# Second attention of a two-block transformer: the last value panel moved behind the query panels and cut in two halves, the orders of TensorE, VectorE and ScalarE around it rewritten

## The chip, the cores and the metric

The kernel runs on one core of one Trainium2 chip. The metric is the device time in microseconds (us); less is better. A core has five engines that work through separate queues and meet at semaphores: TensorE (PE, matrix products, with its weight loads shown as PEld), VectorE (DVE), ScalarE (ACT), GpSimd (POOL) and SyncE (SP, which here only issues transfers).

## The reference, cut to what matters

The program computes two transformer blocks on 512 tokens of width 1024. The first is a mixer with attention and convolution and a large expert layer. The second, where the change lies, is a sliding-window attention with sinks and a gated feed-forward layer:

```
proj = h @ w_in                                     # 1024 query, 256 key, 256 value columns
s = einsum(q, k) * 64 ** -0.5 - slope * dist        # blocks of 128 queries x 256 keys, 16 heads
m = max(max(s), sink);  p = exp(s - m)
denom = sum(p) + exp(sink - m)
o = einsum(p / denom, v)
x = x + o @ w_out
x = x + swiglu_ffn(rms_norm(x), w_gate_up, w_down)
```

## The kernel before, in words

Every weight matrix comes as panels of 128 x 1024 values. For each panel ScalarE writes a rounded copy (`whi`), VectorE writes the rest (`wlo`, line 1674), and TensorE makes 24 products of 128x128 by 128x512 (lines 551 to 553, three for each of eight slices). `whi` and `wlo` have two slots each. So the copy of panel p waits for the counter `used`, that is for the last product of panel p - 2; in the second attention this copy is `swa_panel_hi(p)` on ScalarE (the activation in line 1096), followed by `swa_panel_lo(p)` on VectorE.

The second attention has twelve panels, numbered 0 to 11 by position: one of keys, one of values, four of queries, the second one of keys, and then before the change the second one of values and four of queries. Its softmax goes through sixteen groups n of four heads and one block of queries; two groups make a pair m. Each group passes through all three engines:

- `swa_scores(m)`, TensorE, line 946: scores of a pair into the PSUM banks 4 to 7. From the second pair on it waits until VectorE has read the whole pair before (`bias2`).
- `bias_tiles(n)`, ScalarE, line 1526: the distance penalty of two heads. VectorE doesn't begin group 0 before the tiles 0 to 3 are there (`dve.wait_ge(bias_ready, NH2 // 2)`).
- `swa_bias(n)`, VectorE, lines 2405 to 2412: scores plus penalty, with the row maxima.
- `swa_exp(n)`, ScalarE, lines 1538 and 1540: the exponentials and their sums.
- `swa_norm(n)`, VectorE, lines 2417 to 2423: division by the sum.
- `swa_turn(n)`, TensorE, line 958: transposes the probabilities. It waits for `swa_norm(n)` and for the copy of the turned group n - 1.
- `swa_out(n)`, ScalarE, line 1548 (for n = 11 `swa_turned` on VectorE, line 2441): copies the turned group out of PSUM.
- `swa_values(m)`, TensorE, line 978, and then `swa_hi(m)` on ScalarE and `swa_lo(m)` on VectorE: the products with the values, stored in two parts.

The groups of the first key panel are n = 0 to 7, those of the second n = 8 to 15. `turn_v` (line 932) transposes a value panel, `value2` and `value2_out` store it. `out_part` makes the first products with `w_out` from the parts that are ready. The order of all this is written out by hand, once for each engine; each engine takes its list from top to bottom and stands still at a wait. The functions that the change touches, and their callers:

Of the kernel before, what the change touches and what calls it, by code (L numbers as in the profile page):

```python
# [28 lines left out]
KT = D // P  # L29
# [24 lines left out]
U = MOD1  # L54
# [20 lines left out]
SPLIT = 2  # L75
BANKS = 4
SWB = (0, 2, 3, 1, 0, 2, 3, 3, 3, 3, 3, 3)
SW_ORDER = (0, 2, 4, 5, 6, 7, 1, 3, 8, 9, 10, 11)
ZEROS = 32
ATT = NH * TT  # L80
DT = TT - 1
# [76 lines left out]
def build(nc, panels, mod2_d, small, xT_d, ctxT_d, rope_d, keys_d, dist_d, w_d, ge_d, out):  # L158
    with ExitStack() as ctx:
# [201 lines left out]
        def r_of(g):  # L361

            return g - U if g < EV else g - U - NK
# [172 lines left out]
        def _(pe):  # L536
# [387 lines left out]
            def swa_panel(p):  # L924
                first = p == 0
                panel(SW + p, p % 4, ps[:, SWB[p], :], a_hi, a_lo, r_of(SW) + (p + 1 if p < 7 else p + 4), (h_ready, 3 * KT) if first else None,
                      (lambda k: norm_stat(3, k, bank=1)) if first else None)

            def turn_v(u, bank):
                pe.wait_ge(v2_feat, u + 1)  # L930
                for s in range(TT):
                    last = pe.transpose(ps[:, bank, s * P:(s + 1) * P], v2_feat_sb[:, u, s * P:(s + 1) * P], ident)
                last.then_inc(v2_turned, 1)
# [3 lines left out]
            def swa_scores(m):  # L937

                b, kt, half = groups[2 * m]
                if m:  # L940
                    pe.wait_ge(bias2, 8 * m)
                for r in range(4):
                    for half in range(2):
                        rows_ = slice(half * HD2, (half + 1) * HD2)
                        dst = ps[:, 4 + 2 * half + r // 2, (r % 2) * 256 + (P if b == 0 else 0):(r % 2) * 256 + 256]
                        last = pe.matmul(dst, q2[rows_, kt * 4 + r, b * P:(b + 1) * P],
                                         k2[rows_, kt, max(b - 1, 0) * P:(b + 1) * P], start=True, stop=True)
                last.then_inc(sc2, 1)

            def swa_turn(n):  # L950
                b, kt, half = groups[n]
                tiles = (1,) if b == 0 else (0, 1)
                pe.wait_ge(pn2, n + 1)
                if n:
                    pe.wait_ge(ptc2, n)
                for s in tiles:
                    for r in range(4):
                        last = pe.transpose(ps[:, s, r * P:(r + 1) * P], s2[:, n % 6, r * 256 + s * P:r * 256 + (s + 1) * P], ident)
                last.then_inc(pt2, 1)

            def swa_values(m):

                b, kt, half = groups[2 * m]
                tiles = (1,) if b == 0 else (0, 1)
                pe.wait_ge(ptc2, 2 * m + 2)
                if m == 0:
                    pe.wait_ge(v2_done, 2)
                elif m < 3:
                    pe.wait_ge(o2, m)
                else:  # L970
                    pe.wait_ge(o2, m - 1)
                if m == 3:
                    pe.wait_ge(bank_free, r_of(SW) + 16)
                for s in tiles:
                    for half in range(2):
                        rows_ = slice(half * HD2, (half + 1) * HD2)
                        kv = 2 * kt + half
                        last = pe.matmul(ps[rows_, values_bank(m), :], v2[:, b - 1 + s, kv * HD2:(kv + 1) * HD2],
                                         p2T[:, 2 * ((2 * m + half) % 3) + s, :],
                                         start=(s == tiles[0]), stop=(s == 1))  # L980
                last.then_inc(pv2, 1)


            def out_part(u, first, count):

                if first == 0:
                    pe.wait_ge(lo_ready, SO + u + (1 - U))
                    pe.wait_ge(bank_free, r_of(SO) + u + 1)
                    pe.wait_ge(bias2, 4 * len(groups))
                    pe.wait_ge(o2, TT)  # L990
                if first == 4:
                    pe.wait_ge(o2, 2 * TT)
                for k in range(first, first + count):
                    last = split3(ps[:, 4 + u, :], u, k, b_hi[:, k, :], b_lo[:, k, :], k == 0, k == KT - 1)
                if first == 4:
                    last.then_inc(used, 1)
# [16 lines left out]
            swa_scores(1)  # L1013
            swa_panel(8)
            swa_turn(0)
            turn_v(1, 2)
            swa_scores(2)
            swa_turn(1)
            swa_panel(9)
            swa_turn(2)  # L1020
            swa_values(0)
            swa_scores(3)
            swa_turn(3)
            swa_panel(10)
            swa_turn(4)
            swa_values(1)
            swa_turn(5)
            swa_panel(11)
            swa_turn(6)
            pe.wait_ge(bank_free, r_of(SW) + 16)  # L1030
            swa_scores(4)
            swa_values(2)
            swa_turn(7)
            swa_scores(5)
            swa_values(3)
            swa_scores(6)
            swa_turn(8)
            swa_turn(9)
            swa_scores(7)
            swa_values(4)  # L1040
            swa_turn(10)
            swa_turn(11)
            out_part(0, 0, 2)
            swa_values(5)
            swa_turn(12)
            out_part(0, 2, 2)
            swa_turn(13)
            out_part(1, 0, 2)
            swa_values(6)
            swa_turn(14)  # L1050
            out_part(1, 2, 1)
            swa_turn(15)
            out_part(1, 3, 1)
            swa_values(7)
            out_part(0, 4, 4)
            out_part(1, 4, 4)
            for k in range(2, KT):
# [33 lines left out]
        def _(act):  # L1091
# [464 lines left out]
            for n in range(3):  # L1556
                bias_tiles(n)
                swa_panel_hi(6 + n)
            bias_tiles(3)
            bias_tiles(4)  # L1560
            swa_exp(0)
            swa_panel_hi(9)
            swa_exp(1)
            swa_exp(2)
            swa_panel_hi(10)
            swa_out(0)
            swa_exp(3)
            swa_out(1)
            swa_exp(4)
            swa_exp(5)  # L1570
            swa_panel_hi(11)
            swa_out(2)
            swa_hi(0)
            swa_out(3)
            bias_tiles(5)
            swa_exp(6)
            swa_out(4)
            swa_panel_hi(12)
            swa_hi(1)
            swa_exp(7)  # L1580
            swa_out(5)
            bias_tiles(6)
            bias_tiles(7)
            swa_out(6)
            swa_hi(2)
            swa_out(7)
            swa_exp(8)
            swa_exp(9)
            swa_hi(3)
            swa_exp(10)  # L1590
            swa_out(8)
            swa_exp(11)
            swa_out(9)
            swa_exp(12)
            swa_exp(13)
            hi_next(0, SO, 0)
            swa_hi(4)
            swa_out(10)
            swa_exp(14)
            swa_exp(15)  # L1600
            swa_hi(5)
            swa_out(12)
            swa_out(13)
            swa_hi(6)
            swa_out(14)
            swa_out(15)
            swa_hi(7)

# [60 lines left out]
        def _(dve):  # L1669
# [759 lines left out]
                dve.tensor_tensor(b_lo[:, kt * 4:kt * 4 + 4, at], ps[:, values_bank(m), :].rearrange("p (r t) -> p r t", r=4),  # L2429
                                  f32(b_hi[:, kt * 4:kt * 4 + 4, at]), ALU.subtract).then_inc(o2, 1)  # L2430

            def pair_bias(m):
                swa_bias(2 * m)
                swa_bias(2 * m + 1)

            def swa_turned(n):
                dve.wait_ge(pt2, n + 1)
                dve.wait_ge(pv2, (n - 3) // 2 + 1)
                first = 1 if groups[n][0] == 0 else 0
                to = 2 * (n % 3)  # L2440
                dve.tensor_copy(p2T[:, to + first:to + 2, :], ps[:, first:2, :]).then_inc(ptc2, 1)

            def pair_norm(m):
                swa_norm(2 * m)
                swa_norm(2 * m + 1)

            query2(2, 4)
            dve.tensor_scalar(less_sinks[:, :], col("sinks", 0, NH2), -1.0, None, ALU.mult).then_inc(fold_g, 1)
# [6 lines left out]
            swa_panel_lo(8)  # L2455
            dve.wait_ge(fold_g, 3)
            dve.wait_ge(bias_ready, NH2 // 2)
            pair_bias(0)
            value2(1, 7)
            swa_panel_lo(9)  # L2460
            pair_bias(1)
            pair_norm(0)
            query2(4, 8)
            swa_panel_lo(10)
            value2_out(1, 2)
            pair_bias(2)
            pair_norm(1)
            query2(5, 9)
            swa_panel_lo(11)
            pair_norm(2)  # L2470
            swa_lo(0)
            pair_bias(3)
            query2(6, 10)
            residual(4, 4)
            swa_panel_lo(12)
            swa_lo(1)
            pair_norm(3)
            query2(7, 11)
            dve.wait_ge(bias_ready, NH2)
            pair_bias(4)  # L2480
            swa_lo(2)
            pair_bias(5)
            pair_norm(4)
            swa_lo(3)
            pair_bias(6)
            pair_norm(5)
            pair_bias(7)
            swa_lo(4)
            swa_turned(11)
            pair_norm(6)  # L2490
            lo_next(0, SO, 0)
            swa_lo(5)
            pair_norm(7)
            swa_lo(6)
            swa_lo(7)

# [216 lines left out]
```

## Time and profile before

| | |
|---|---|
| median of 3 runs | 2474.28 us (2472.31 to 2475.38) |
| profiled execution, time | 2492.27 us |
| profiled execution, span from first to last instruction | 2490.5 us |
| TensorE busy in the span | 97% |
| VectorE, ScalarE, GpSimd busy | 68%, 38%, 30% |
| granted TensorE clock, mean | 0.990 |

The span is the time from the first to the last instruction of the one profiled execution; 1.8 us lie around it. The busy share counts an engine as busy while an instruction runs on it; times of instructions are from the start of the span. The second attention begins at about 1942 us of it and ends, with its output panels, at about 2114 us. The granted clock is 1.00 for 2.4 GHz and 0.50 for 1.2 GHz.

### The profile page before, as it was taken

The page shows a single profiled execution, that of the slowest core. Times are in us where ns is not written, and L with a number is a line of the kernel's source. Part 1 is how long each engine was busy: PE and PEld are TensorE (multiplying, and loading weights), DVE is VectorE, ACT ScalarE, POOL GpSimd, SP SyncE. Part 2 cuts the span into 40 slices and gives each one's busy share as a digit, 9 for nine tenths or more (in the row PEclk, how much of TensorE's full clock was granted, in tenths as well). Part 3 has the DMA queues.
Part 4 walks back from the last instruction along what each step waited for, and adds up shares of the span by engine and source line. Part 5 has one row for each costly group of instructions (what it writes and reads, how often), then busy time and mean ns, then how long its engine had stood idle before and what let it go on. Part 6 is the DMA issues. An engine that isn't in the chain of part 4 may idle for free.

```text
span 2490.5 us, 34880 instructions
## 1 busy us (share of the span) xinstructions
PE 2420.3 (97%) x11986; PEld 2062.4 (83%) x11986; DVE 1696.0 (68%) x3261; ACT 935.0 (38%) x1436; POOL 741.3 (30%) x646
## 2 busy tenths in 40 slices
PE   6999999998999999999999999999999989999998
PEld 5887787786888887888888899999999767888886
DVE  4987878787667776778632378888888785444434
ACT  5225842523233333333333333333333474222232
POOL 0000000000036665667675357777741000000000
PEclk9999999998999999999999999999999999999999
DMA  6235813453244444444445689999998212232321
GB/s 270 93 98 186 283 60 127 160 190 132 90 156 143 140 152 135 144 144 148 132 148 181 225 281 365 360 365 359 359 360 292 70 43 68 93 100 93 97 97 68
DMA packets 179146, 436.26 MB, mean 175 GB/s; under 512 B 33392, under 2 KB 82544, under 8 KB 178672
## 3 DMA queue, kind: packets, MB, share of 16 engines
q1 hardware_dynamic: 123984, 331.74, 39.1%
q0 software_dynamic: 34816, 67.41, 7.7%
q10 hardware_dynamic: 20256, 36.06, 3.9%
q8 instruction: 38, 0.62, 0.1%
q14 instruction: 52, 0.43, 0.1%
HBM read 371.48 MB, written 61.01 MB: 174 GB/s over the span
## 4 chain that ended last, share of the span: by engine, by line
PE 83%; DVE 7%; issue 1%; ACT 1%; another core or an unknown queue 1%; ACTq 0%; DVEq 0%
PE ps L551 17%; PE ps L553 17%; PE ps L552 17%; PE ps L897 9%; PE ps L895 9%; PE ps L896 8%; DVE ar L1727 1%; PE ps L794 1%; DVE wlo L1674 1%; PE ps L760 1%; PE ps L869 1%; DVE ar L1789 1%; DVE tiny L1903 1%; PE ps L784 1%
## 5 line engine op out<-in xcount | busy, mean ns | idle before, releaser
L2610 POOL DMA_INDIRECT w_scratch<-ar x384 | 419.2, 1092 | 932.1 <-DVE wlo L2122 823.5
L551 PE MATMUL ps<-b_hi,whi 128*128 128x512 f32 x1312 | 513.3, 391 | 4.6 <-DVE wlo L2120 4.4
L553 PE MATMUL ps<-b_hi,wlo 128*128 128x512 f32 x1312 | 511.5, 390 | 0.0
L552 PE MATMUL ps<-b_lo,whi 128*128 128x512 f32 x1312 | 511.1, 390 | 0.0
L1674 DVE TENSOR_TENSOR wlo<-raw,whi 128x1024 fp32r<-128x1024 f32 x235 | 287.4, 1223 | 272.7 <-ACT whi L1096 203.4
L895 PE MATMUL ps<-a_hi,whi 128*128 128x384 f32 x1016 | 340.8, 335 | 7.5 <-DVE a_lo L2304 5.2
L896 PE MATMUL ps<-a_lo,whi 128*128 128x384 f32 x1016 | 340.2, 335 | 0.4 <-issue 0.4
L897 PE MATMUL ps<-a_hi,wlo 128*128 128x384 f32 x1016 | 340.2, 335 | 0.2 <-issue 0.2
L551 PE MATMUL ps<-a_hi,whi 128*128 128x512 f32 x808 | 322.1, 399 | 0.9 <-DVEq L1884 0.6
L553 PE MATMUL ps<-a_hi,wlo 128*128 128x512 f32 x808 | 315.1, 390 | 0.0
L552 PE MATMUL ps<-a_lo,whi 128*128 128x512 f32 x808 | 315.1, 390 | 0.0
L551 PEld LDWEIGHTS ps<-b_hi,whi 128*128 128x128 f32 x1312 | 246.8, 188 | 57.4 <-issue 6.1
L553 PEld LDWEIGHTS ps<-b_hi,wlo 128*128 128x128 f32 x1312 | 246.5, 188 | 51.6
L552 PEld LDWEIGHTS ps<-b_lo,whi 128*128 128x128 f32 x1312 | 246.8, 188 | 50.9
L1096 ACT ACTIVATE whi<-raw 128x1024 fp32r<-128x1024 f32 x168 | 177.2, 1055 | 294.6 <-PE ps L553 183.4
L2588 POOL DMA_INDIRECT ar<-panels,ar x128 | 150.5, 1176 | 173.3 <-DVE nt L2320 97.7
L895 PEld LDWEIGHTS ps<-a_hi,whi 128*128 128x128 f32 x1016 | 191.4, 188 | 8.9 <-DVE a_lo L2304 5.5
L896 PEld LDWEIGHTS ps<-a_lo,whi 128*128 128x128 f32 x1016 | 191.4, 188 | 1.4 <-issue 1.4
L897 PEld LDWEIGHTS ps<-a_hi,wlo 128*128 128x128 f32 x1016 | 191.3, 188 | 0.0
L2595 POOL DMA_INDIRECT ar<-gelu_scratch,ar x128 | 171.1, 1337 | 49.4 <-issue 38.7
L551 PEld LDWEIGHTS ps<-a_hi,whi 128*128 128x128 f32 x808 | 152.1, 188 | 37.4 <-issue 4.4
L552 PEld LDWEIGHTS ps<-a_lo,whi 128*128 128x128 f32 x808 | 152.0, 188 | 33.5 <-issue 2.9
(298 smaller groups left out, 3470.2 us busy)
## 6 DMA issues: line engine op xcount, KB each, us to landing
raw<-panels SPq DMA_DIRECT2D x302, 512.0 KB
late<-panels SPq DMA_DIRECT2D x128, 512.0 KB
w_scratch<-rstd SPq DMA_DIRECT2D x32, 768.0 KB, 10.7
ar<-w_scratch SPq DMA_DIRECT2D x128, 192.0 KB
ar<-gelu_scratch SPq DMA_DIRECT2D x128, 192.0 KB
ar<-mod SPq DMA_DIRECT2D x32, 512.0 KB
gelu_scratch<-ar ACTq DMA_DIRECT2D x64, 256.0 KB
gelu_scratch<-sq ACTq DMA_DIRECT2D x32, 256.0 KB
```

The source lines that it names most:

```text
L551: pe.matmul(bank, w_h, hi[:, k, :], start=(k == 0), stop=False)
L552: pe.matmul(bank, w_h, lo[:, k, :], start=False, stop=False)
L553: last = pe.matmul(bank, w_l, hi[:, k, :], start=False, stop=(k == KT - 1))
L760: pe.matmul(ps[:, b, :], qT[:, h, t * P:(t + 1) * P], kT[:, hu, 0:T], start=True, stop=True)
L895: pe.matmul(ps[:, d, 0:cols], w_h, hi[:, at, 0:cols], start=first, stop=False)
L896: pe.matmul(ps[:, d, 0:cols], w_h, lo[:, at, 0:cols], start=False, stop=False)
L897: end = pe.matmul(ps[:, d, 0:cols], w_l, hi[:, at, 0:cols], start=False, stop=last)
L1096: act.activation(whi[:, u % SPLIT, :], raw[:, u % RAW, :], ACT.Copy).then_inc(hi_ready, 1)
L1674: dve.tensor_tensor(wlo[:, u % SPLIT, :], src, f32(whi[:, u % SPLIT, :]), ALU.subtract).then_inc(lo_ready, 1)
L2588: nc.gpsimd.indirect_dma_start(v_rows[:, s % VS, :], None, v_table, bass.IndirectOffsetOnAxis(vals[:, column(s)].bitcast(U32), 0)).then_in ...
L2595: nc.gpsimd.indirect_dma_start(g_pick[:, s:s + 1], None, gelus_, bass.IndirectOffsetOnAxis(offs[:, column(s)], 0)).then_inc(gpick_in[h % 2 ...
L2610: nc.gpsimd.indirect_dma_start(experts, bass.IndirectOffsetOnAxis(offs[:, k:k + 1], 0), vals[:, k:k + 1], None)\
```

## The change

The value panel that stood at position 7 now stands at position 11, the query panels move up by one, and TensorE makes its products in two halves (`last_value_half`) with scores and a transpose between them. `turn_v(1, ...)` and with it the store of the values move behind them. The value product of pair 0 waits only for the first value panel, that of pair 3 for both. Beside this all three lists have a new order. The diff, cut:

```diff
-SW_ORDER = (0, 2, 4, 5, 6, 7, 1, 3, 8, 9, 10, 11)
+SW_ORDER = (0, 2, 4, 5, 6, 7, 1, 8, 9, 10, 11, 3)
...
                 if m == 0:
-                    pe.wait_ge(v2_done, 2)
+                    pe.wait_ge(v2_done, 1)
...
                 if m == 3:
-                    pe.wait_ge(bank_free, r_of(SW) + 16)
+                    pe.wait_ge(v2_done, 2)
...
+            def last_value_half(half):
+
+                if half == 0:
+                    pe.wait_ge(lo_ready, SW + 11 + (1 - U))
+                    pe.wait_ge(bank_free, r_of(SW) + 15)
+                for k in range(4 * half, 4 * half + 4):
+                    last = split3(ps[:, SWB[11], :], 3, k, a_hi[:, k, :], a_lo[:, k, :], k == 0, k == KT - 1)
+                if half:
+                    last.then_inc(used, 1)
```

TensorE's list from the second scores to the second output panel, the part that changes:

```diff
             swa_scores(1)
             swa_panel(8)
             swa_turn(0)
-            turn_v(1, 2)
             swa_scores(2)
             swa_turn(1)
             swa_panel(9)
+            swa_scores(3)
             swa_turn(2)
             swa_values(0)
-            swa_scores(3)
             swa_turn(3)
             swa_panel(10)
             swa_turn(4)
+            pe.wait_ge(bank_free, r_of(SW) + 15)
+            swa_scores(4)
             swa_values(1)
+            last_value_half(0)
+            swa_scores(5)
             swa_turn(5)
-            swa_panel(11)
+            last_value_half(1)
             swa_turn(6)
-            pe.wait_ge(bank_free, r_of(SW) + 16)
-            swa_scores(4)
             swa_values(2)
             swa_turn(7)
-            swa_scores(5)
-            swa_values(3)
+            turn_v(1, 3)
             swa_scores(6)
             swa_turn(8)
+            swa_values(3)
             swa_turn(9)
             swa_scores(7)
+            swa_turn(10)
             swa_values(4)
-            swa_turn(10)
             swa_turn(11)
-            out_part(0, 0, 2)
+            out_part(0, 0, 4)
...
```

ScalarE's list, its first part:

```diff
             for n in range(3):
                 bias_tiles(n)
                 swa_panel_hi(6 + n)
+            swa_panel_hi(9)
             bias_tiles(3)
+            swa_panel_hi(10)
             bias_tiles(4)
             swa_exp(0)
-            swa_panel_hi(9)
             swa_exp(1)
+            bias_tiles(5)
             swa_exp(2)
-            swa_panel_hi(10)
             swa_out(0)
+            swa_panel_hi(11)
             swa_exp(3)
             swa_out(1)
             swa_exp(4)
             swa_exp(5)
-            swa_panel_hi(11)
+            bias_tiles(6)
             swa_out(2)
...
```

VectorE's list, its first part (`pair_bias(m)` was `swa_bias(2 * m)` and `swa_bias(2 * m + 1)`, `pair_norm` likewise):

```diff
             dve.wait_ge(bias_ready, NH2 // 2)
-            pair_bias(0)
-            value2(1, 7)
+            swa_bias(0)
+            swa_bias(1)
+            query2(4, 7)
+            swa_norm(0)
+            swa_bias(2)
+            swa_bias(3)
+            swa_norm(1)
+            query2(5, 8)
             swa_panel_lo(9)
-            pair_bias(1)
-            pair_norm(0)
-            query2(4, 8)
+            swa_norm(2)
+            swa_bias(4)
+            swa_bias(5)
             swa_panel_lo(10)
-            value2_out(1, 2)
-            pair_bias(2)
-            pair_norm(1)
-            query2(5, 9)
+            residual(4, 1)
+            query2(6, 9)
+            swa_norm(3)
...
```

Three places in the built order. First ScalarE where the copies of the panels 8, 9 and 10 stand (`whi<-raw`), with the penalty tiles (`ar<-ar,sm`), the table load and the exponentials of group 0 and 1 (the rows that wait for `nmx2`). Before:

```order
L1096 ACTIVATE whi<-raw 128x1024 [waits used,landed0]
L1526 ACTIVATE ar<-ar,sm 128x256 x4
L1538 ACT_TABLE_LOAD
L1538 ACTIVATE ar,tiny<-ar,tiny 128x256 [waits nmx2]
L1538 ACTIVATE ar,tiny<-ar,tiny 128x256 x3
L1540 ACTIVATE tiny<-tiny 128x4
L1096 ACTIVATE whi<-raw 128x1024 [waits used,landed1]
L1538 ACTIVATE ar,tiny<-ar,tiny 128x256 [waits nmx2]
```

The same place of the change, where lines stand ten numbers further down (line 1106 is 1096 of before, 1536 is 1526, 1548 is 1538):

```order
L1106 ACTIVATE whi<-raw 128x1024 [waits used,landed0]
L1106 ACTIVATE whi<-raw 128x1024 [waits used,landed1]
L1536 ACTIVATE ar<-ar,sm 128x256 x2
L1106 ACTIVATE whi<-raw 128x1024 [waits used,landed2]
L1536 ACTIVATE ar<-ar,sm 128x256 x2
L1548 ACT_TABLE_LOAD
L1548 ACTIVATE ar,tiny<-ar,tiny 128x256 [waits nmx2]
L1548 ACTIVATE ar,tiny<-ar,tiny 128x256 x3
L1550 ACTIVATE tiny<-tiny 128x4
```

The copy of panel 9 moved ahead of the tiles of `bias_tiles(3)`, and that of panel 10 ahead of `bias_tiles(4)` and of the first exponential. Second place, ScalarE behind the third group: the copy out of PSUM of group 0 (waits for `pt2`), and the copy of panel 11. Before:

```order
L1096 ACTIVATE whi<-raw 128x1024 [waits used,landed2]
L1548 ACTIVATE ar<-ps 128x1024 [waits pt2]
L1538 ACTIVATE ar,tiny<-ar,tiny 128x256 [waits nmx2]
L1538 ACTIVATE ar,tiny<-ar,tiny 128x256 x3
L1540 ACTIVATE tiny<-tiny 128x4
L1548 ACTIVATE ar<-ps 128x1024 [waits pt2]
```

And of the change (line 1558 is 1548 of before):

```order
L1558 ACTIVATE ar<-ps 128x1024 [waits pt2]
L1106 ACTIVATE whi<-raw 128x1024 [waits used,landed3]
L1548 ACTIVATE ar,tiny<-ar,tiny 128x256 [waits nmx2]
L1548 ACTIVATE ar,tiny<-ar,tiny 128x256 x3
L1550 ACTIVATE tiny<-tiny 128x4
L1558 ACTIVATE ar<-ps 128x1024 [waits pt2]
```

The copy of panel 11 now stands ahead of the exponentials of group 3 and the copy out of group 1, where it stood behind group 5 before. Third place, TensorE in the second half of the attention, from `swa_turn(7)` to `swa_scores(7)`. Before:

```order
L958 MATMUL ps<-sm,ar 128x128 x3
L946 MATMUL ps<-ar 128x256 [waits bias2]
L946 MATMUL ps<-ar 128x256 x7
L978 MATMUL ps<-ar 64x512 [waits bank_free,o2,ptc2]
L978 MATMUL ps<-ar 64x512
L946 MATMUL ps<-ar 128x256 [waits bias2]
L946 MATMUL ps<-ar 128x256 x7
L958 MATMUL ps<-sm,ar 128x128 [waits ptc2,pn2]
L958 MATMUL ps<-sm,ar 128x128 x7
L958 MATMUL ps<-sm,ar 128x128 [waits ptc2,pn2]
L958 MATMUL ps<-sm,ar 128x128 x7
L946 MATMUL ps<-ar 128x128 [waits bias2]
```

And of the change:

```order
L958 MATMUL ps<-sm,ar 128x128 x3
L932 MATMUL ps<-sm,nt 128x128 [waits v2_feat]
L932 MATMUL ps<-sm,nt 128x128 x3
L946 MATMUL ps<-ar 128x256 [waits bias2]
L946 MATMUL ps<-ar 128x256 x7
L958 MATMUL ps<-sm,ar 128x128 [waits ptc2,pn2]
L958 MATMUL ps<-sm,ar 128x128 x7
L978 MATMUL ps<-ar 64x512 [waits v2_done,o2,ptc2]
L978 MATMUL ps<-ar 64x512
L958 MATMUL ps<-sm,ar 128x128 [waits ptc2,pn2]
L958 MATMUL ps<-sm,ar 128x128 x7
L946 MATMUL ps<-ar 128x128 [waits bias2]
```

`swa_scores(5)` has left this place for one between the halves of the value panel, and of the four rows of scores and value products that followed each other two transposes now stand between.

## Rows read from the trace of the kernel before

**Rows 1.** The page: busy time, share of the span and instructions of TensorE.

```profile
PE 2420.3 (97%) x11986; PEld 2062.4 (83%) x11986; DVE 1696.0 (68%) x3261; ACT 935.0 (38%) x1436; POOL 741.3 (30%) x646
```

**Rows 2.** Windows: length, then busy time of PE, PEld, DVE, ACT, POOL; PEclk; DMA.

```profile
1989.23:2019.08 29.85, 29.85 (x182) 23.04 (x181) 26.62 (x88) 23.29 (x67) 0.00 (x0) 1.00 0.20 68
2019.08:2081.59 62.51, 52.88 (x291) 34.45 (x290) 43.25 (x150) 39.65 (x120) 0.00 (x0) 0.97 0.07 22
```

**Rows 3.** Waits from 2034 to 2077 us: waiting line, releaser, total, times, longest.

```profile
PE ps L946 <- DVE tiny L2405: 5.4, 3, 2.4
...
PE ps L958 <- ACT ar L1548: 2.4, 2, 1.2
...
PE ps L623 <- DVE b_lo L2429: 1.4, 1, 1.4
```

**Rows 4.** Timeline of ScalarE: start, duration, line, operands, idle before and its releaser.

```profile
1989.39 1.06 ACT L1096 ACTIVATE whi<-raw 128x1024 fp32r<-128x1024 f32 x1 [3.58 <-PE ps L553]
1990.36 1.70 ACT L1526 ACTIVATE ar<-ar,sm 128x256 f32<-128x256 f32 x4
1992.07 1.28 ACT L1538 ACT_TABLE_LOAD   x1
1993.51 0.51 ACT L1538 ACTIVATE ar<-ar,tiny 128x256 f32<-128x256 f32 x1 [0.16 <-DVE tiny L2412]
...
1995.50 0.19 ACT L1540 ACTIVATE tiny<-tiny 128x4 f32<-128x4 f32 x1
1997.03 1.06 ACT L1096 ACTIVATE whi<-raw 128x1024 fp32r<-128x1024 f32 x1 [1.34 <-PE ps L553]
...
2004.66 1.06 ACT L1096 ACTIVATE whi<-raw 128x1024 fp32r<-128x1024 f32 x1 [1.34 <-PE ps L553]
2005.63 1.01 ACT L1548 ACTIVATE ar<-ps 128x1024 f32<-128x1024 f32 x1
```

**Rows 5.** Timeline of VectorE, groups 0 and 1 and the copy of panel 10.

```profile
1991.63 0.42 DVE L2405 CUSTOM_DVE_ANT_0 ar<-ps,ar 128x256 f32<-128x256 f32 x1
...
1994.77 0.08 DVE L2405 DVE_READ_ACCUMULATOR2_ANT tiny<- 128x1 f32 x1
...
2002.80 0.15 DVE L2417 TENSOR_TENSOR tiny<-tiny 128x4 f32<-128x4 f32 x1
...
2003.20 1.23 DVE L2423 TENSOR_TENSOR ar<-ar,tiny 128x1024 f32<-128x1024 f32 x1
2004.35 0.15 DVE L2417 TENSOR_TENSOR tiny<-tiny 128x4 f32<-128x4 f32 x1
...
2006.49 1.21 DVE L1674 TENSOR_TENSOR wlo<-raw,whi 128x1024 fp32r<-128x1024 f32 x1
```

**Rows 6.** Timeline of TensorE from the second scores to panel 10.

```profile
1996.86 2.00 PE L946 MATMUL ps<-ar 64*128 64x256 f32 x16
...
2004.48 1.09 PE L958 MATMUL ps<-sm,ar 128*128 128x128 f32 x8
2005.41 0.60 PE L932 MATMUL ps<-sm,nt 128*128 128x128 f32 x4
2005.94 0.49 PE L946 MATMUL ps<-ar 64*128 64x256 f32 x2
...
2008.72 0.47 PE L551 MATMUL ps<-a_hi,whi 128*128 128x512 f32 x1
...
2019.08 0.47 PE L551 MATMUL ps<-a_hi,whi 128*128 128x512 f32 x1
```

**Rows 7.** Windows at half clock in this stage, and at half and full clock elsewhere.

```profile
2054.20:2057.50 3.30, 3.30 (x8) 0.65 (x8) 3.16 (x14) 3.30 (x14) 0.00 (x0) 0.50 0.00 0
...
1428.64:1432.64 4.00, 4.00 (x12) 4.00 (x13) 2.72 (x4) 0.52 (x1) 0.00 (x0) 0.50 0.85 281
1433.09:1437.00 3.91, 3.91 (x24) 3.91 (x24) 0.83 (x1) 1.47 (x2) 0.00 (x0) 1.00 0.39 140
```

**Rows 8.** Timeline of TensorE: the idle time ahead of the second window of rows 7.

```profile
1428.64 0.69 PE L895 MATMUL ps<-a_hi,whi 128*128 128x384 f32 x1 [5.18 <-DVE a_lo L2304]
```

More of the change, by code:

```diff
@@ L1025, in _ @@
             swa_turn(4)
+            pe.wait_ge(bank_free, r_of(SW) + 15)
+            swa_scores(4)
             swa_values(1)
+            last_value_half(0)
+            swa_scores(5)
             swa_turn(5)
-            swa_panel(11)
+            last_value_half(1)
             swa_turn(6)
-            pe.wait_ge(bank_free, r_of(SW) + 16)
-            swa_scores(4)
             swa_values(2)
             swa_turn(7)
-            swa_scores(5)
-            swa_values(3)
+            turn_v(1, 3)
             swa_scores(6)
             swa_turn(8)
+            swa_values(3)
             swa_turn(9)
             swa_scores(7)
+            swa_turn(10)
             swa_values(4)
-            swa_turn(10)
             swa_turn(11)
-            out_part(0, 0, 2)
+            out_part(0, 0, 4)
+            swa_turn(12)
             swa_values(5)
-            swa_turn(12)
-            out_part(0, 2, 2)
             swa_turn(13)
             out_part(1, 0, 2)
+            swa_turn(14)
             swa_values(6)
-            swa_turn(14)
+            swa_turn(15)
             out_part(1, 2, 1)
-            swa_turn(15)
+            swa_values(7)
             out_part(1, 3, 1)
-            swa_values(7)
             out_part(0, 4, 4)
@@ L1570, in _ @@
             swa_exp(5)
-            swa_panel_hi(11)
+            bias_tiles(6)
             swa_out(2)
+            swa_exp(6)
+            bias_tiles(7)
             swa_hi(0)
             swa_out(3)
-            bias_tiles(5)
-            swa_exp(6)
+            swa_exp(7)
             swa_out(4)
@@ L1579, in _ @@
             swa_hi(1)
-            swa_exp(7)
+            swa_exp(8)
+            swa_exp(9)
             swa_out(5)
-            bias_tiles(6)
-            bias_tiles(7)
+            swa_exp(10)
             swa_out(6)
@@ L1586, in _ @@
             swa_out(7)
-            swa_exp(8)
-            swa_exp(9)
+            swa_exp(11)
+            swa_out(8)
             swa_hi(3)
-            swa_exp(10)
-            swa_out(8)
-            swa_exp(11)
             swa_out(9)
             swa_exp(12)
+            swa_out(10)
+            swa_hi(4)
+            hi_next(0, SO, 0)
             swa_exp(13)
-            hi_next(0, SO, 0)
-            swa_hi(4)
-            swa_out(10)
             swa_exp(14)
-            swa_exp(15)
-            swa_hi(5)
             swa_out(12)
             swa_out(13)
+            swa_exp(15)
+            swa_out(14)
+            swa_hi(5)
             swa_hi(6)
-            swa_out(14)
             swa_out(15)
@@ L2430, in swa_lo @@
                                   f32(b_hi[:, kt * 4:kt * 4 + 4, at]), ALU.subtract).then_inc(o2, 1)
-            def pair_bias(m):
-                swa_bias(2 * m)
-                swa_bias(2 * m + 1)
             def swa_turned(n):
@@ L2441, in swa_turned @@
                 dve.tensor_copy(p2T[:, to + first:to + 2, :], ps[:, first:2, :]).then_inc(ptc2, 1)
-            def pair_norm(m):
-                swa_norm(2 * m)
-                swa_norm(2 * m + 1)
             query2(2, 4)
@@ L2457, in _ @@
             dve.wait_ge(bias_ready, NH2 // 2)
-            pair_bias(0)
-            value2(1, 7)
+            swa_bias(0)
[6 more added lines that the diff above has]
+            query2(5, 8)
             swa_panel_lo(9)
-            pair_bias(1)
-            pair_norm(0)
-            query2(4, 8)
+            swa_norm(2)
+            swa_bias(4)
+            swa_bias(5)
             swa_panel_lo(10)
-            value2_out(1, 2)
-            pair_bias(2)
-            pair_norm(1)
-            query2(5, 9)
+            residual(4, 1)
+            query2(6, 9)
+            swa_norm(3)
+            swa_bias(6)
             swa_panel_lo(11)
-            pair_norm(2)
+            swa_norm(4)
+            swa_bias(7)
+            swa_norm(5)
             swa_lo(0)
-            pair_bias(3)
-            query2(6, 10)
-            residual(4, 4)
-            swa_panel_lo(12)
[L2476 to L2480, printed above, removed]
+            query2(7, 10)
+            swa_norm(6)
+            swa_norm(7)
+            dve.wait_ge(bias_ready, NH2)
+            swa_bias(8)
+            swa_bias(9)
+            swa_lo(1)
+            swa_panel_lo(12)
+            swa_norm(8)
+            swa_bias(10)
+            swa_norm(9)
+            value2(1, 11)
+            swa_bias(11)
+            swa_norm(10)
+            value2_out(1, 3)
             swa_lo(2)
-            pair_bias(5)
-            pair_norm(4)
+            swa_bias(12)
+            swa_bias(13)
+            swa_norm(11)
+            swa_bias(14)
             swa_lo(3)
-            pair_bias(6)
-            pair_norm(5)
-            pair_bias(7)
+            swa_bias(15)
+            swa_norm(12)
+            swa_turned(11)
+            lo_next(0, SO, 0)
+            swa_norm(13)
             swa_lo(4)
-            swa_turned(11)
-            pair_norm(6)
-            lo_next(0, SO, 0)
+            swa_norm(14)
+            residual(5, 3)
+            swa_norm(15)
             swa_lo(5)
-            pair_norm(7)
             swa_lo(6)
```

## The prediction

> **What bounds the kernel now.** I read the page first: TensorE is busy 97% of the span [rows 1], so only what lengthens or fills TensorE's queue counts, and the question is where in the second attention it stands still. The windows answer that. From the second key panel's end to the start of panel 10 (1989.23 to 2019.08) TensorE is busy all of 29.85 us; from there to the end of the eighth slice of the second output panel (2019.08 to 2081.59) it is busy 52.88 of 62.51 us [rows 2]. So before the change the first half has no gap at all, and the second has 62.51 - 52.88 = 9.63 us of them. The waits name them: scores behind VectorE's row maxima 5.4 us, transposes behind ScalarE's copies 2.4, the output panel behind the last `swa_lo` 1.4 [rows 3]. To this comes a stretch of 3.30 us at half clock with TensorE busy all through, which costs half of it, 1.65 us [rows 7]. More than 9.6 + 1.7 = 11.3 us the change cannot win here. ScalarE's timeline then says what the first half lives on: the copies of the panels 9 and 10 start at 1997.03 and 2004.66, each after idle time that ended with the last product of a panel [rows 4]. They cannot come earlier, since only then is a slot of `whi` free. All that ScalarE has to do for the softmax before that is done in between: four penalty tiles and the table load from 1990.36 on, and the first exponentials by 1995.69 [rows 4].
>
> **The first half, step by step.** I lay the new lists out with the durations of before; times are on the clock of before, and the profiled execution serves for all of them.
>
> 1. ScalarE's copy of panel 9 now stands ahead of `bias_tiles(3)`. It starts at 1997.03 as before and hands on 0.97 us later (1989.39 to 1990.36); two tiles are half of 1.70 us. The tiles 0 to 3, for which VectorE waits, are complete at 1998.9 instead of by about 1991.2.
> 2. VectorE's groups 0 and 1 took from 1991.63 to 1994.85, 3.22 us [rows 5]. They now end at 2002.1, and `swa_scores(1)`, at 1996.86 before [rows 6], waits for them: **a stall of 5.3 us**. VectorE had hidden its 3.2 us behind panel 7; now nothing covers them.
> 3. Scores and panel 8 take the 7.8 us from 1996.86 to 2004.66 [rows 4, 6]. The panel ends at 2009.9, and ScalarE, idle since 1998.9, copies panel 10 then, because this copy stands ahead of `bias_tiles(4)` and of the first exponential. Copy 0.97, tiles 0.85, table load 1.28, group 0 from 1993.51 to 1995.69, 2.18 us [rows 4]: ready at 2015.3.
> 4. `swa_norm(0)` takes from 2002.80 to 2004.43, 1.63 us [rows 5], so `swa_turn(0)` goes at 2017.0 against 2004.48 [rows 6]: **a stall of 7.1 us**, 12.5 us late in sum.
> 5. `swa_scores(2)` needs group 3's maxima, and on VectorE these stand behind norm 0 now: 2015.3 + 1.55 + 3.22 = 2020.1, while the transpose is over 0.93 us after 2017.0 [rows 5, 6]. **2.2 us**.
> 6. Behind that on VectorE stand norm 1 (1.55), a query store (0.6, what lies between norm 1's end at 2005.9 and the copy at 2006.49) and `swa_panel_lo(9)` (1.2, as that copy) [rows 5]. Panel 9 can go at 2023.7; scores (1.93) and a transpose (0.93) fill until 2022.9: **0.8 us**. Before it began at 2008.72 [rows 6].
> 7. Panel 9 ends 5.6 us later, at 2029.3. Only then can ScalarE copy panel 11, which now stands ahead of the exponentials of group 3 and the copy out of group 1, for which `swa_turn(2)` waits. 0.97 + 2.1 + 0.95 us [rows 4] put that transpose at 2033.4, and the short scores in front of it end at about 2030.3: **3.2 us**.
> 8. `swa_turn(3)` waits for the copy of group 2, behind two exponentials (4.2 us), two tiles (0.85) and the copy itself (1.0): 2039.4. The transpose before and `swa_values(0)` take some 2.8 of these 6.0 us: **3.2 us**. Panel 10 begins at 2040.3, against 2019.08 [rows 6].
>
> The stalls make 21.8 us. From the first half `turn_v(1)` is gone (2005.41 to 2005.94, 0.53 us [rows 6]), which leaves 21.2 us, the distance of the two starts of panel 10.
>
> **The second half.** From panel 10 on both versions make the same products (the two halves are 24 products too), plus the 0.5 us of `turn_v(1)`. The work is 62.51 - 9.63 - 1.65 = 51.2 us. Taken in the same way, row by row, the new list waits little: scores 4 and 5 stand where VectorE has had a whole panel half or more to empty the banks, and the value products and transposes alternate. I find gaps of 0.2, 0.35, 0.1, 0.1 and at the end 0.8 us before the last slices, which wait for `swa_lo(7)` as before; in sum 1.7 us (bounds 0 and the 9.63 of before, since those are the same instructions between the same engines; nearer the low end, as ScalarE and VectorE are busy 39.65 and 43.25 of 62.51 us [rows 2], with room). So the stage ends at 2040.3 + 51.2 + 0.5 + 1.7 = 2093.7, against 2081.6: **+12.1 us**. The change in this half does what it looks laid out for and gives back 9.63 + 1.65 - 1.7 = 9.6 us; the first half takes twice that.
>
> **Clock.** Stalls as long as these have a second price. After 5.18 us without a product [rows 8] the granted clock stood at 0.50, and the next 12 products took 4.00 us where 24 take 3.91 later [rows 7]: 2.0 us lost. Nothing is lost where the clock recovers while TensorE waits anyway. Two stalls of the change are as long or longer; the first hits panel 8, which the whole chain hangs on, in full; the second falls partly into the wait of step 5. Bounds 0 and 4 us, I take 2. So +12.1 + 2 = **+14 us**: span 2504.5 instead of 2490.5. The profiled execution took 2492.27 us, 0.7% over the median of 2474.28; the difference is taken over to the median unscaled: **2488 us**.
>
> **Rules of the Trainium skill.** By "PSUM — Partial Sum Buffer", section "Engine vs sequencer instructions", the queues of ScalarE and VectorE are strict FIFO. That speaks against this change, since nothing behind a waiting panel copy could run, and the trace agrees: the two copies in rows 4 begin only when the panel ends, and what is written behind them comes after. Did the queue let ready tiles pass, the steps 1 to 4 would vanish. By "TensorE: Matmul & The Clock Gate", Part 1, an idle engine falls back to 1.2 GHz and activity releases it; taken strictly for both long stalls, the sum would be +16 instead of +14 us.
>
> **Rivals.** (a) *The second half doesn't recover*, because VectorE now handles groups one by one between stores, or because half clock lasts over several stalls: half of the 9.63 us stays, or another 4 us at half clock. +18 to +22 us, 2492 to 2496. For it speaks that VectorE has 43 us of work in this half whatever the order; against it, that the waits of rows 3 come from scores asked for right behind each other, which the new list pulls apart. (b) *The first half stalls less*: ready work on ScalarE or VectorE makes up 4 to 8 us of the chain, +5 to +10 us, 2479 to 2484. Against it: each link in the steps 1 to 5 is a list position and a measured duration, and the engines are idle ahead of it. (c) *Faster or equal*: `swa_panel_hi(9)` and `(10)` find their slot free before the panel ends, so tiles and exponentials are not held up. Then the stalls of the steps 1 to 6 (15.4 us) fall away and 12.1 - 15.4 = -3 us stay, 2471; without those of the steps 7 and 8 (6.4 us) too it is -9.7, 2465. It turns where the stalls of the first half make 9.7 us in sum. Against it stands the release of both copies by the last product of a panel [rows 4].
>
> **How the numbers follow.** The forecast 0.78 (its own range 2484 to 2492), (a) 0.08, (b) 0.07, (c) 0.07, half of it within 0.2% and half faster. Within 0.2%, about 5 us, is what a measurement of this kernel can't tell from no change. All but (c) are slower by more: 0.92 slower, 0.04 same, 0.04 faster. The range 2483 to 2493 takes the edges of (a) and (b) in: below, less clock loss (-2) and shorter chains (-3); above, the full clock loss (+2) and 3 us of gaps in the second half.
>
> **What would show it.** In the profile after: ScalarE's tiles of step 1 right behind a panel copy near 1998, and nothing on ScalarE from there to about 2010; TensorE idle some 5 us ahead of the second scores, released by VectorE, and 7 us ahead of the first transpose; two gaps of about 3 us before the transposes 2 and 3, released by ScalarE's copies; a stretch of granted clock 0.50 in panel 8; hardly a gap above 0.5 us from panel 10 on; the last slices of the second output panel some 14 us later. The forecast is wrong if ScalarE's first exponentials still come near 1994, or if the gaps of the second half are still there.

## The result

The changed kernel takes 2490.02 us (median of 4 runs, 2488.36 to 2491.09) against 2473.89 us before (4 runs), a ratio of 1.0063 with a 95% interval of 1.0052 to 1.0075: 16.1 us slower. The forecast was 2488 us, 14 us slower.

The spans of the two profiled executions don't show this: 2487.2 us after, 2490.5 before. The execution of before that was profiled was 18 us longer than its own median, and it had lost that time ahead of the changed stage, where the programs are the same: its first scores start at 1989.2 us, those of the changed kernel at 1970.6. Of these 18.6 us 11.7 are more idle time of TensorE and 6.9 more busy time; the wait of [rows 8], 5.18 us, is a part of them, and the trace of the changed kernel doesn't have it. What made them is not shown. So below I compare the stage alone, from the first scores to the end of the eighth slice of the second output panel. Windows of the changed kernel, columns as in [rows 2]; the first two answer to the two windows there, the third is their sum:

```profile
1970.60:2025.38 54.78, 36.62 (x177) 27.00 (x177) 29.30 (x108) 24.98 (x76) 0.00 (x0) 0.81 0.12 42
2025.38:2078.36 52.98, 51.81 (x295) 34.70 (x294) 40.49 (x130) 37.51 (x113) 0.00 (x0) 1.00 0.06 21
...
1970.60:2078.36 107.76, 88.43 (x469) 61.70 (x469) 69.80 (x237) 62.49 (x187) 0.00 (x0) 0.90 0.09 32
```

The same stage before, in one window:

```profile
1989.20:2081.59 92.39, 82.76 (x469) 57.49 (x469) 69.90 (x237) 62.94 (x187) 0.00 (x0) 0.98 0.11 37
```

The stage grew from 92.4 to 107.8 us, by 15.4 us, all but 0.8 of what the median grew by, which is well inside the interval of that (12.9 to 18.6 us). Up to panel 10 it took 54.8 instead of 29.85 us, 24.9 more; behind it 53.0 instead of 62.5, 9.5 less. TensorE's idle time went from 9.6 to 19.3 us (+9.7), and its busy time from 82.8 to 88.4 (+5.7) with the same 469 products: that is work at half clock.

ScalarE's timeline of the changed kernel, the rows that answer to [rows 4]. Line 1106 is the panel copy, 1536 the penalty tiles, 1548 the exponentials, 1558 the copy of turned probabilities:

```profile
1970.73 1.06 ACT L1106 ACTIVATE whi<-raw 128x1024 fp32r<-128x1024 f32 x1 [3.58 <-PE ps L553]
1978.36 1.06 ACT L1106 ACTIVATE whi<-raw 128x1024 fp32r<-128x1024 f32 x1 [6.58 <-PE ps L553]
1979.32 0.89 ACT L1536 ACTIVATE ar<-ar,sm 128x256 f32<-128x256 f32 x2
1993.47 1.06 ACT L1106 ACTIVATE whi<-raw 128x1024 fp32r<-128x1024 f32 x1 [13.25 <-PE ps L553]
1994.43 0.89 ACT L1536 ACTIVATE ar<-ar,sm 128x256 f32<-128x256 f32 x2
1995.34 1.28 ACT L1548 ACT_TABLE_LOAD   x1
...
2014.55 1.06 ACT L1106 ACTIVATE whi<-raw 128x1024 fp32r<-128x1024 f32 x1 [9.21 <-PE ps L553]
```

Three times ScalarE stands at a panel copy until TensorE's last product of the panel before last (L553), for 6.6, 13.3 and 9.2 us. The work that it has ready is written behind the copy. What TensorE does meanwhile, from its timeline ([rows 6] before; the count of a row is of the part of a group that fell into the window asked for):

```profile
1983.64 1.65 PE L946 MATMUL ps<-ar 64*128 64x256 f32 x6 [5.38 <-DVE tiny L2415]
...
1987.35 0.79 PE L551 MATMUL ps<-a_hi,whi 128*128 128x512 f32 x1
2000.52 1.97 PE L958 MATMUL ps<-sm,ar 128*128 128x128 f32 x8 [7.15 <-DVE ar L2433]
2003.67 1.65 PE L946 MATMUL ps<-ar 64*128 64x256 f32 x6 [1.17 <-DVE tiny L2415]
2008.75 0.48 PE L551 MATMUL ps<-a_hi,whi 128*128 128x512 f32 x1
2018.72 1.52 PE L958 MATMUL ps<-sm,ar 128*128 128x128 f32 x6 [3.17 <-ACT ar L1558]
2024.56 0.63 PE L958 MATMUL ps<-sm,ar 128*128 128x128 f32 x4 [1.28 <-ACT ar L1558]
```

The row names VectorE as the releaser of the two long stalls. It is only the last link: VectorE itself waited, as its own timeline says, for ScalarE's penalty tiles (L1536) and for the first exponentials (L1550):

```profile
1980.35 0.42 DVE L2415 CUSTOM_DVE_ANT_0 ar<-ps,ar 128x256 f32<-128x256 f32 x1 [7.31 <-ACT ar L1536]
...
1998.83 0.17 DVE L2427 TENSOR_TENSOR tiny<-tiny 128x4 f32<-128x4 f32 x1 [14.25 <-ACT tiny L1550]
```

So the chain runs from the end of a panel over ScalarE's copy, ScalarE's softmax work and VectorE back to TensorE. The granted clock in three windows of the changed kernel:

```profile
1981.20:1988.10 6.90, 4.46 (x18) 3.19 (x19) 3.24 (x17) 0.00 (x0) 0.00 (x0) 0.51 0.01 2
1998.30:2008.50 10.20, 6.80 (x30) 5.23 (x30) 9.32 (x31) 6.44 (x24) 0.00 (x0) 0.50 0.00 0
2018.80:2022.20 3.40, 3.40 (x12) 1.99 (x14) 3.26 (x15) 3.40 (x16) 0.00 (x0) 0.51 0.01 2
```

20.5 us stand at 0.5 (1.2 GHz), each stretch with a stall in it or ahead of it, where before the change there were 3.3 us of it in the stage ([rows 7]). In them TensorE was busy 14.7 us, which at full clock is about 7.3 us of work.

### The profile page after: what moved, and what is told of

Same layout as the page of the kernel before. It is cut to its first block, busy times and chain, and to the rows that moved or that the text cites. A ratio compares the mean times of both kernels' runs of the same rounds, so it can differ in the third digit from the quotient of the medians.

```text
span 2487.2 us, 34880 instructions
## 1 busy us (share of the span) xinstructions
PE 2419.1 (97%) x11986; PEld 2063.7 (83%) x11986; DVE 1697.8 (68%) x3261; ACT 937.5 (38%) x1436; POOL 733.4 (29%) x646
## 4 chain that ended last, share of the span: by engine, by line
PE 84%; DVE 6%; ACT 2%; issue 1%; DVEq 0%; ACTq 0%
PE ps L551 17%; PE ps L553 17%; PE ps L552 17%; PE ps L895 9%; PE ps L896 9%; PE ps L897 9%; DVE ar L1737 1%; PE ps L794 1%; DVE wlo L1684 1%; PE ps L760 1%; PE ps L869 1%; PE ps L946 1%; DVE ar L1799 1%; DVE tiny L1913 1%; PE ps L784 1%
## 5 line engine op out<-in xcount | busy, mean ns | idle before, releaser
L2629 POOL DMA_INDIRECT w_scratch<-ar x384 | 412.3, 1074 | 929.3 <-DVE wlo L2132 833.7
L553 PE MATMUL ps<-b_hi,wlo 128*128 128x512 f32 x1312 | 511.1, 390 | 0.0
L553 PE MATMUL ps<-a_hi,wlo 128*128 128x512 f32 x800 | 311.8, 390 | 0.0
L553 PEld LDWEIGHTS ps<-b_hi,wlo 128*128 128x128 f32 x1312 | 246.4, 188 | 51.4
```

What stands on the lines that cost most here:

```text
L553: last = pe.matmul(bank, w_l, hi[:, k, :], start=False, stop=(k == KT - 1))
L2629: nc.gpsimd.indirect_dma_start(experts, bass.IndirectOffsetOnAxis(offs[:, k:k + 1], 0), vals[:, k:k + 1], None)\
```

## The experiments

Three chips were used. On two of them the kernel before ran at 2500 and 2510 us with a spread of some 20 us, so for the experiments there the stage of the profile carries the verdict; it repeats well (the kernel with all three copies moved back was profiled on two chips: 82.42 and 82.38 us). Stage lengths are from the first scores to the end of the eighth slice of the second output panel throughout. A ratio is to the kernel before, timed on the same chip, with its 95% interval; it is not the quotient of the two medians and differs from it by up to 0.1%.

**1. The two tiles ahead of the first copy.** The changed kernel, ScalarE's list:

```diff
-            swa_panel_hi(9)
             bias_tiles(3)
+            swa_panel_hi(9)
             swa_panel_hi(10)
             bias_tiles(4)
```

> The changed kernel with one move: the two penalty tiles that VectorE waits for stand ahead of ScalarE's copy of panel 9 again. The stage (from the first scores to the end of the second output panel) took 92.4 us before and 107.8 us after the change. Theory (a panel copy at the head of ScalarE's list holds up what stands behind it, place by place): the stall of 5.4 us ahead of the second scores goes, and with it the half clock in panel 8; the stall ahead of the first transpose stays at about 7 us. Stage 99 to 102.5 us, 6 to 8 us under the changed kernel, 2482 to 2484 us. Rival (VectorE's new order, or the missing value panel, makes the stalls): no move of more than 1 us, 2489 to 2491.

The window of the stage:

```profile
1992.10:2092.68 100.58, 86.64 (x469) 60.48 (x469) 69.78 (x237) 62.49 (x187) 0.00 (x0) 0.92 0.10 34
```

100.6 us, 7.2 less than the changed kernel; ratio to before 1.0031 (1.0013 to 1.0048). The stall of 5.38 us is gone; the next is there to the hundredth:

```profile
2014.56 1.75 PE L958 MATMUL ps<-sm,ar 128*128 128x128 f32 x7 [7.15 <-DVE ar L2433]
```

One list position of two tiles of 0.45 us costs 5.4 us of stall and, with its clock, 7.2 us. VectorE's order and the missing value panel, unchanged here, don't make it by themselves.

**2. Copies 9 and 10 back.**

```diff
-            swa_panel_hi(9)
             bias_tiles(3)
-            swa_panel_hi(10)
             bias_tiles(4)
             swa_exp(0)
+            swa_panel_hi(9)
             swa_exp(1)
             bias_tiles(5)
             swa_exp(2)
+            swa_panel_hi(10)
             swa_out(0)
             swa_panel_hi(11)
```

> The changed kernel with the copies of panels 9 and 10 on ScalarE back at their places of before, behind the first and the third exponentials; that of panel 11 stays early. Theory: both long stalls and the one ahead of the third scores go, no half clock; two gaps of about 3 us ahead of the transposes 2 and 3 stay. Stage 87 to 89 us, 3.5 to 5.5 us under the kernel before, 2468.5 to 2470.5. Rival (VectorE's order makes part of the front stalls): more than 3 us of waits on VectorE ahead of panel 10, stage above 91 us. Rival (panel copies placed late make panels late): waits of TensorE on the copies' remainders (VectorE's wlo) ahead of panels 9 and 10.

The stage, and in it TensorE's waits of over 0.4 us:

```profile
1993.50:2083.39 89.89, 82.64 (x469) 58.50 (x469) 69.79 (x237) 62.53 (x187) 0.00 (x0) 0.98 0.12 38
```

```profile
PE ps L958 <- ACT ar L1558: 6.3, 3, 3.2
PE ps L623 <- DVE b_lo L2439: 0.5, 1, 0.5
```

89.9 us, 2.5 less than before the change, ratio 0.9982 (0.9961 to 1.0003), so that the times alone don't tell it from before. It is 0.9 us over the expected stage, and the half clock that was expected to be gone is there once more. Both long stalls and that ahead of the third scores are gone, no wait for a copy's remainder came in their place; what is left is 3.17 and 2.90 us ahead of transposes 2 and 3, the price of the early copy of panel 11, and 3.4 us of half clock behind them.

**3. Copy 11 back too.**

```diff
             swa_out(0)
-            swa_panel_hi(11)
             swa_exp(3)
             swa_out(1)
             swa_exp(4)
             swa_exp(5)
+            swa_panel_hi(11)
             bias_tiles(6)
```

> As the kernel with copies 9 and 10 back, and the copy of panel 11 behind group 5's exponentials too. Theory: the two gaps of 3 us ahead of the transposes 2 and 3 go as well; only some 1.5 us of gaps are left in the stage, all of what the second half wins is kept. Stage 81.5 to 83.5 us, 9 to 11 us under the kernel before, 2463 to 2465. Rival (the second half wins only because the long stalls of the first let VectorE and ScalarE work ahead): the gaps of the second half come back, 5 us or more, stage above 87 us.

```profile
1991.20:2073.62 82.42, 81.26 (x469) 57.29 (x469) 69.67 (x237) 62.94 (x187) 0.00 (x0) 1.00 0.12 42
```

82.4 us: 10.0 less than before, 25.3 less than the changed kernel. TensorE is idle for 1.2 us of it, at full clock all through. The gaps of the second half didn't come back, so it had not won them from the stalls ahead of it. The ratio was 0.9971, with a wide interval (0.9950 to 0.9992), so it was timed again:

> The same kernel as e3_copy_11_back, timed again, since the runs of its first comparison spread over 18 us. Its stage was 82.4 us against 92.4 us before the change. Theory (the stage is all that differs): 10 us under the kernel before, ratio 0.9955 to 0.9965. Rival (the win is given back later, for instance in the feed-forward layer): ratio above 0.998.

Ratio 0.9953 (0.9935 to 0.9971), 2500.66 against 2510.2 us on this chip. Behind the stage, to the end of the span, the traces of before and of this kernel both take 408.9 us, so nothing is given back later. It is the fastest version found.

**4. The kernel before with the two copies early.**

```diff
+            swa_panel_hi(9)
             bias_tiles(3)
+            swa_panel_hi(10)
             bias_tiles(4)
             swa_exp(0)
-            swa_panel_hi(9)
             swa_exp(1)
             swa_exp(2)
-            swa_panel_hi(10)
```

> The kernel before with one move: on ScalarE the copy of panel 9 ahead of the penalty tiles 3 and that of panel 10 ahead of the tiles 4 and the first exponentials, as the change has them. Nothing else of the change. Theory: stalls of 5.3 us ahead of the second scores, about 7 ahead of the first transpose and 2 behind it, half clock after them, and the 9.6 us of gaps of the second half unchanged: stage 105 to 110 us, 12 to 17 us over the kernel before, 2486 to 2491. Rival (the stalls come of the other parts of the change): less than 3 us over before.

TensorE's waits up to 2050 us, and the stage:

```profile
PE ps L958 <- DVE ar L2423: 7.2, 1, 7.2
PE ps L946 <- DVE tiny L2405: 5.4, 1, 5.4
```

```profile
2002.60:2111.26 108.66, 85.38 (x469) 60.28 (x469) 70.19 (x237) 62.56 (x187) 0.00 (x0) 0.94 0.09 32
```

108.7 us, 16.3 over before; ratio 1.0066 (1.0046 to 1.0086), about as much as the whole change, which however wins back 9.5 us in its second half. With no other line of the change in it, the kernel has the same two stalls (5.38 and 7.15 us). They need nothing but the two list positions. The wait of about 2 us that was expected behind them didn't come: in the list of before VectorE does the maxima of the second pair ahead of `swa_norm(0)`. Up to panel 10 this kernel took 46.7 us, 16.9 more than before, where the changed kernel took 24.9 more. Experiments 2 and 3 part these the other way round: 18.4 go with the copies 9 and 10 (panel 10 starts 36.4 us behind the first scores), 6.9 with copy 11 (29.5 us).

**5. The stalls filled.** `ones` and the constants of `sm` are multiplied into the empty bank 2; the products are used nowhere.

```diff
+            def fill(n):
+                for _ in range(n):
+                    pe.matmul(ps[:, 2, :], ones, sm[:, 0:T], start=True, stop=True)
...
             swa_panel(7)
+            fill(5)
             swa_scores(1)
             swa_panel(8)
+            fill(7)
             swa_turn(0)
+            fill(2)
             swa_scores(2)
...
             swa_scores(3)
+            fill(3)
             swa_turn(2)
```

> The changed kernel with idle products of ones and constants into an empty bank in TensorE's stalls: 5 ahead of the second scores, 7 ahead of the first transpose, 2 ahead of the third scores, 3 ahead of the transpose of group 2, 0.86 us each, a little less than each stall. They compute nothing that is used. Theory (half clock is a price of its own on top of the stalls): no stretch of half clock, the stage is 2.5 to 4 us shorter than the changed kernel's 107.8, 103.8 to 105.3 us, time 2486 to 2487.5. Rival (the clock loss hides in the waits): no difference, or longer by what the products overrun.

The stage, and a part of it around the one gap that was not filled:

```profile
1972.10:2078.01 105.91, 98.25 (x503) 64.57 (x503) 69.75 (x237) 62.48 (x187) 0.00 (x0) 0.98 0.10 32
...
2022.00:2029.00 7.00, 6.38 (x25) 5.26 (x26) 2.67 (x8) 5.93 (x23) 0.00 (x0) 0.76 0.08 32
```

And from TensorE's timeline the third scores, the start of panel 9 and `swa_turn(3)` (line numbers stand eight further down than in the changed kernel):

```profile
2003.12 2.00 PE L946 MATMUL ps<-ar 64*128 64x256 f32 x16 [0.33 <-DVE tiny L2423]
2006.79 0.50 PE L551 MATMUL ps<-a_hi,whi 128*128 128x512 f32 x1 [0.64 <-DVE wlo L1692]
2022.62 1.07 PE L958 MATMUL ps<-sm,ar 128*128 128x128 f32 x8 [2.89 <-ACT ar L1566]
```

105.9 us, 1.9 less than the changed kernel and 0.6 over what was expected (2487.66 us, ratio 1.0052, 1.0035 to 1.0068). The half clock behind the filled stalls is gone, but one stretch of 3.4 us came behind a wait that was not filled, ahead of `swa_turn(3)`, and that wait is 2.89 us where it was 1.28. Both readings are partly right. Panel 10 starts 51.35 us behind the first scores (2023.45), 3.4 earlier than the 54.78 of the changed kernel; behind that point the filled kernel takes 54.56 instead of 52.98 us, 1.6 more, because its half clock now lies where nothing waits. And part of the lost speed had indeed been hidden, since a slow transpose and a slow `swa_values(0)` had used up the wait behind them. The two better parts would make 51.35 + 52.98 = 104.3 us together; that is an estimate, since no run has both. By it the clock costs about 3.4 us of the stage of the changed kernel.

**6. The new lists in the second half alone.** The kernel before up to the scores of pair 5, from there the three lists of the change; the value panel stays at position 7. TensorE's part:

```diff
             swa_scores(5)
-            swa_values(3)
             swa_scores(6)
             swa_turn(8)
+            swa_values(3)
             swa_turn(9)
             swa_scores(7)
-            swa_values(4)
             swa_turn(10)
+            swa_values(4)
             swa_turn(11)
...
```

> The kernel before, value panel and everything up to the scores of pair 5 as it was, with the three lists of the change from there on (value products and transposes alternate, groups one by one). Theory (what the second half wins comes mostly from the value panel as cover between the scores, and a smaller part from the order): the stall ahead of the scores of pair 6 grows to about 6 us, the later ones go, in sum 2 us less of gaps and the half clock perhaps elsewhere; stage 89 to 92.5 us, 0 to 3.5 us under the kernel before, 2470.5 to 2474. Rival (the order alone makes the win): 7 us or more under before.

Waits in the stage:

```profile
PE ps L946 <- DVE tiny L2404: 7.1, 2, 6.1
PE ps L623 <- DVE b_lo L2428: 0.5, 1, 0.5
PE ps L946 <- DVE ar L2373: 0.3, 1, 0.3
```

91.1 us, 1.3 less than before, 2473.64 us, ratio 0.9997 (0.9987 to 1.0007). The late waits are gone and one of 6.1 us stands ahead of the scores of pair 6, with half clock behind it. The order of these lists alone wins little.

**7. The value panel in one piece**, in the kernel of experiment 3:

```diff
-            last_value_half(0)
             swa_scores(5)
             swa_turn(5)
+            last_value_half(0)
             last_value_half(1)
             swa_turn(6)
```

> As the kernel with the copies 9, 10 and 11 back, but with the last value panel in one piece behind the scores of pair 5 and transpose 5, not in halves around them. Theory (where the panel stands matters, the halves little): one gap of about 1.5 us ahead of the scores of pair 5 more, stage 83 to 85.5 us, 1 to 2 us longer than the kernel with halves. Rival (the halves are what wins): 4 us or more longer.

```profile
PE ps L946 <- DVE tiny L2415: 1.9, 2, 1.6
```

83.9 us, 1.4 more than with the halves around the scores and the transpose; 2466.55 us, ratio 0.9969 (0.9956 to 0.9981). The 1.6 us are one wait ahead of the scores of pair 5.

## Why the prediction was right

The direction, the place and the mechanism held, and the time lies 2 us above the forecast. The span did not come out as forecast: 2487.2 instead of 2504.5 us, because the profiled execution of before had lost 18.6 us ahead of the stage, and that of the changed kernel had not. The forecast took only the difference over to the median, and the difference is what held. By its steps:

- Steps 1 and 2: a stall of 5.3 us was forecast, 5.38 measured. Experiment 1 takes it away with two tiles, experiment 4 makes it with the copies.
- Steps 3 and 4: 7.1 forecast, 7.15 measured, with the table load and the first exponentials behind the copy of panel 10 as laid out.
- Step 5: 2.2 forecast, 1.17 measured; step 6: 0.8 forecast, none measured; step 8: 3.2 forecast, 1.28 measured. In each a piece of TensorE's work at half clock ran into the wait and used it up. The forecast had laid these waits out at full clock, and at full clock, in experiment 5, they are there: third scores 2.2 us behind the transpose (0.33 of it left idle, the rest filled), 0.64 ahead of panel 9, 2.89 ahead of `swa_turn(3)`. (The terms written out in step 6 add up to 2023.5, not 2023.7; the trace has 0.3 us more than they do, two short operations of VectorE behind the maxima.)
- Step 7: 3.2 forecast, 3.17 measured.
- The first half in sum: 21.2 us at full clock and 2 for the clock were forecast, 24.9 measured. With the stalls filled it was 51.35 - 29.85 = 21.5. The mis-sized term is the clock: by experiment 5 about 3.4 us instead of 2. The changed kernel's own trace says where: the second scores took 3.71 us instead of 1.93 and panel 8 another 0.2 more, and panel 9 began at 2008.75, when VectorE's remainder for it had been ready since 2007.3. Without the clock 104.3 - 92.4 = 11.9 us are left, against the forecast 12.1.
- The second half: 1.7 us of gaps forecast, 52.98 - 51.81 = 1.17 measured. It gives back 9.5 us (9.1 forecast, the difference of 62.5 and 53.4). Experiment 3 shows that they don't hang on the stalls of the first half. The new lists of the last part alone give 1.3 us (experiment 6), the halves 1.4 (experiment 7). That most of it comes from the last value panel standing between scores is what is left over; no run moved the panel without the lists around it, so it is argued and not shown.

Rival (c), that the change is no loss, turns on whether the copies of panels 9 and 10 hold up what stands behind them, and experiments 2 and 3 come near to what it would have been: 2.5 us less than before with these two copies out of the way, where the forecast had worked out 3, and 10.0 less without that of panel 11 too, where it had 9.7. Rival (a) fell with the gaps of the second half. Of rival (b) nothing was seen.

ScalarE stood 13.25 us at a copy, with tiles behind it that wait for nobody and exponentials whose maxima VectorE had finished by 1982.2, 11 us before the copy began. That agrees with the Trainium skill, "PSUM — Partial Sum Buffer", section "Engine vs sequencer instructions": strict FIFO queues. The rule on the clock of the Trainium skill, "TensorE: Matmul & The Clock Gate", Part 1, by which an idle engine falls back to 1.2 GHz, taken strictly for both long stalls, gave +16, nearer to the 15.4 and 16.1 than the middle value that I took.

What stays open: what of the second half's win is the value panel's place, why the profiled execution of the kernel before was 18 us over its median, and why two chips ran the same kernel at 2500 to 2510 us.

## What to carry to other kernels

Where an engine serves two streams from one list by hand, here weight panels and softmax, put a step whose release is far off behind everything that is ready sooner: a panel copy that can't start before a panel ends cost nothing late here (experiment 3) and held up both streams early. A wait that names one engine is often the end of a chain; follow the releaser's own wait before blaming it. And compare the stage, not the span, when two profiled executions are set side by side: here the slower kernel had the shorter span.

## What the hardware showed beyond that

Of the 20.5 us at half clock, TensorE's busy time tells 5.7 us more than before the change, but by experiment 5 it costs only about 3.4 us of time: here the work at half speed that ended in a wait cost nothing. A stall of 1.3 us in a profile with half clock ahead of it was one of 2.9 us at full clock.
